# Moving three positions in the issue order of a hybrid attention and expert-retrieval layer: ScalarE's stage work, one weight load, three transposes

## The reference, cut to what matters

```python
# mixer: differential attention and causal pooling, merged by gates
h = x @ w_in                                  # q, k, v, p (pooling input), g (gates)
a = softmax(q1 k1) - lam * softmax(q2 k2)     # 8 heads, causal, ALiBi bias
attn = rms_norm(a @ v) @ w_attn_proj
pool = (multiscale_pool(p) @ pool_w) * pool_scale @ w_pool_proj
h1 = layer_norm(ALPHA * x + (g_attn * attn + g_pool * pool) @ w_out)
# PEER: 8 heads choose 16 of 16384 experts for each token
s = (h1 @ w_q) . sub_keys                     # two halves of 128 scores for each head
idx, gate = top-16 of the sums of two top-16 lists, softmax
act = gelu(u[idx] . h1)
out = layer_norm(ALPHA * h1 + sum(gate * act * v[idx]))
```

## Time and profile before

| | |
|---|---|
| median of 3 runs | 3181.0 us (3175.33 to 3182.49) |
| the profiled execution, its own time | 3174.81 us |
| its span in the trace | 3173.0 us |
| mean granted TensorE clock | 0.959 |
| PE busy | 2873.1 us (91%) |
| DVE busy | 2479.3 us (78%) |
| ACT busy | 964.8 us (30%) |
| POOL busy | 920.2 us (29%) |
| chain that ended last | PE 61%, DVE 20%, DMA 12%, issue 4%, ACT 2% |

### The profile page before, as it was taken

One profiled execution on the slowest core, in us unless ns is written; L12 is line 12 of the kernel. 1 busy time (PEld: TensorE's weight loads), 2 busy tenths in 40 slices (PEclk: granted clock), 3 DMA queues, 4 the chain that ended last, 5 costly groups with the idle time before them and its releaser, 6 DMA issues.

```text
span 3173.0 us, 31535 instructions
## 1 busy us (share of the span) xinstructions
PE 2873.1 (91%) x9793; PEld 1685.4 (53%) x9793; DVE 2479.3 (78%) x5164; ACT 964.8 (30%) x2683; POOL 920.2 (29%) x866
## 2 busy tenths in 40 slices
PE   9999999997698888967988888888999999999997
PEld 7785666553354555533555656333455545555553
DVE  2114678889898999899879998677877878877877
ACT  2311466611224556411235644111111111111110
POOL 1101234433333445433100012222333333333331
PEclk9999999998899999998999988999999999999999
DMA  5735889899999889899646479999999999999995
GB/s 184 256 105 188 325 301 338 311 393 364 417 392 360 326 303 332 328 408 381 250 138 235 164 258 340 390 386 394 414 398 406 403 394 404 392 413 413 402 404 196
DMA packets 225446, 1047.41 MB, mean 330 GB/s; under 512 B 23424, under 2 KB 70016, under 8 KB 141440
## 3 DMA queue, kind: packets, MB, share of 16 engines
q0 software_dynamic: 92160, 671.13, 53.9%
q1 hardware_dynamic: 132112, 374.13, 31.9%
q10 hardware_dynamic: 1008, 0.14, 0.0%
HBM read 995.50 MB, written 49.81 MB: 329 GB/s over the span
## 4 chain that ended last, share of the span: by engine, by line
PE 61%; DVE 20%; DMA 12%; issue 4%; ACT 2%; SPq 1%; POOL 0%; DVEq 0%; POOLq 0%; ACTq 0%
PE w_ps L1901 15%; PE w_ps L1669 12%; PE r_o L1915 12%; PE w_ps L1915 6%; DVE z_e L1556 5%; DVE ring L1598 4%; PE r_o L1847 3%; PE r_o L1669 3%; DMA ring<-uv,idx 3%; DMA gel_kept<-e_scr 2%; DVE hot_r L1478 2%; PE w_ps L1809 1%; DMA ub<-uT 1%; PE w_ps L1847 1%; PE r_o L1754 1%
## 5 line engine op out<-in xcount | busy, mean ns | idle before, releaser
L919 POOL DMA_INDIRECT ring<-uv,idx x640 | 762.6, 1192 | 1937.5 <-DVE z_e L1556 1872.0
L1556 DVE SCALAR_TENSOR_TENSOR z_e<-ring,coef,z_e 128x1024 f32<-128x1024 f32 x640 | 818.4, 1279 | 202.5 <-ACT coef L1153 202.1
L1598 DVE CUSTOM_DVE_ANT_0 ring<-ring,ytok 128x1024 f32<-128x1024 f32 x640 | 777.7, 1215 | 20.5 <-DMA ring<-uv,idx 20.1
L1901 PE MATMUL w_ps<-yT,ub 128*128 128x384 f32 x2048 | 693.3, 493 | 7.6 <-DMA ub<-uT 7.6
L1901 PEld LDWEIGHTS w_ps<-yT,ub 128*128 128x128 f32 x2048 | 393.6, 194 | 297.5 <-issue 52.6
L1669 PE MATMUL w_ps<-x,w 128*128 128x384 f32 (+1 forms) x1632 | 487.2, 446 | 8.2 <-DMA x<-xT 6.2
L1669 PEld LDWEIGHTS w_ps<-x,w 128*128 128x128 f32 x1632 | 303.5, 192 | 146.9 <-issue 26.8
L1915 PE MATMUL r_o<-vb,gel_d 128*128 128x512 f32 x704 | 318.2, 595 | 4.8 <-DMA vb<-v 4.8
L1130 ACT ACTIVATE gel_d<-w_ps 128x384 f32<-128x384 f32 x92 | 45.1, 490 | 767.4 <-PE w_ps L1901 767.4
L1149 ACT ACTIVATE gel<-dot 128x2 f32<-128x2 f32 x320 | 64.0, 200 | 645.9 <-DVE dot L1598 645.3
L1915 PEld LDWEIGHTS r_o<-vb,gel_d 128*128 128x128 f32 x704 | 134.4, 191 | 155.9 <-issue 127.2
(11 more groups left out here) (251 smaller groups left out, 3306.7 us busy)
## 6 DMA issues: line engine op xcount, KB each, us to landing
w<-w_in SPq DMA_DIRECT2D x132, 512.0 KB, 5.4
ub<-uT SPq DMA_DIRECT2D x128, 512.0 KB, 7.9
vb<-v SPq DMA_DIRECT2D x128, 512.0 KB, 9.9
g_scr<-stage_g SPq DMA_DIRECT2D x12, 2048.0 KB, 7.3
gq<-g_scr SPq DMA_DIRECT2D x16, 1536.0 KB, 24.7
wq<-wq SPq DMA_DIRECT2D x46, 512.0 KB, 7.8
wc<-w_branch SPq DMA_DIRECT2D x24, 768.0 KB, 8.4
wo<-w_out SPq DMA_DIRECT2D x24, 512.0 KB, 11.7
```

What stands on the lines that cost most here:

```text
L919: nc.gpsimd.indirect_dma_start(out=ring[t % RING][:], out_offset=None, in_=a["uv"], in_offset=bass.IndirectOffsetOnAxis(ap=idx[:, slot:slo ...
L1556: nc.vector.scalar_tensor_tensor(z[n % 2][:], ring[t % RING][:, D:], coef[:, slot:slot + 1], z[n % 2][:], ALU.mult, ALU.add).then_inc(vsum ...
L1598: nc.vector.tensor_tensor_reduce(ring[r][:, 0:D], ring[r][:, 0:D], y_of(n)[:], 1.0, 0.0, ALU.mult, ALU.add, dot[:, slot:slot + 1]).then_in ...
L1901: ins = nc.tensor.matmul(dense_bank(b)[:, 0:DENSE], ub[b % NUB][:, c], yT[2][c // 4][:, c % 4, :], start=c == 0, stop=c == DC - 1)
```

## The change

```diff
@@ SyncE, tokens(g) @@
             else:
-                yield norm_at(1, GTS[1]) + 15
+                yield score_at(1, 5)
                 sp.wait_ge(y1_out, 16 * len(PARKED))
             sp.dma_start(pw_raw[g][:], a["pool_w"]).then_inc(pw_in, 16)
@@ ScalarE, the loop over the slots @@
             for slot in range(0, SLOTS, GROUP):
                 coefficients(n, slot)
-                advance(tick_at(SLOTS * n + slot + GROUP))
+                advance(tick_at(SLOTS * n + slot + GROUP) + 5)
@@ TensorE, rcg_turns @@
             for i in range(DT):
-                yield TURN_AT[i]
+                yield TURN_AT[i] + 2
                 pe.wait_ge(share_step, 2 * i + 2)
```

## The result

The changed kernel takes **3271.4 us** (median of 4 runs, 3269.6 to 3276.3) against 3178.2 us for the kernel before in the same series. The ratio is 1.0295, with an interval of 1.0279 to 1.0310: about 94 us slower, 89 to 99. The forecast was 3230 us. The direction was right; the loss is nearly twice the forecast's 49 us.

The account below looks back on a forecast made before the run. VectorE was taken to bound stage 2's attention, stage 1's scores and the gate table, TensorE stage 1's attention and the tail. Terms 42 + 6 - 4 + 5 = +49 us on 3181.0 gave 3230 us, range 3178 to 3285.

Parts of the forecast that it names:

- Attention of stage 2, +42 us: Stage 2's attention: exponentials ahead of coefficients make VectorE wait, 34 us in 11 steps and 8 us in 6.
- the lower end: Stage 2's attention: VectorE's 25.5 idle us swallow part of the 42 us of new waits, leaving 16.5 us.
- the upper end: Stage 2's attention: ScalarE's 34.6 us of waits for value products are all handed on, growing it by 77 us.
- the one worked step: Stage 2's attention, slot 202: VectorE's add waits for its coefficient, 3.0 us late, 3.6 with two copies in between.
- Attention of stage 1, +6 us: Stage 1's attention: 14 us of late coefficients, covered by VectorE's idle time; gain at most 6.8, loss up to 28.
- Pooling weights, -4 us: Scores ahead of stage 2's attention: the later load frees SyncE's queue and shortens TensorE's wait; ends -12.1 and +3 us.
- Transpositions, +5 us: Transpositions of the shares: VectorE waits some 5.2 us longer at the first tile, nothing late at others; ends 0 and +5.
- Tail, 0 (-3 to +3): Dense tail: TensorE bounds it and VectorE has 200 us to spare, so ScalarE's lead costs nothing.
- Absorbed: Attention of stage 2: late coefficients fit VectorE's idle time and freed waits gain 19 us, giving 3162 us; chance 0.15.
- everything cancels: Whole kernel: 16.5 us left in stage 2's attention offset by 19 us won elsewhere, giving 3179 us; chance 0.09.
- The window is too narrow: Both attentions: TensorE's lateness passes through ScalarE to VectorE and back, +116 us, giving 3297 us; chance 0.14.
- the forecast's own case: Whole kernel: the summed terms hold, +49 us to 3230 us, within 3195 to 3265; chance 0.62.

Follow-up runs that it names:

- three ticks: Kernel before with ScalarE's work issued three ticks ahead everywhere, nothing else changed; ratio 0.9999 to the kernel before.
- five ticks, one slot more: Kernel before with ScalarE five ticks ahead and VectorE adding each slot one slot later (LAG 4 instead of 3); ratio 0.9991 to the kernel before.
- no table loads: Kernel before with ScalarE five ticks ahead and tanh replacing GELU in gather slots below 252, so output differs; ratio 1.0061 to the kernel before.
- four ticks: Kernel before with ScalarE's work issued four ticks ahead everywhere, nothing else changed; ratio 1.0050 to the kernel before.
- exponentials two ahead: Kernel before with ScalarE five ticks ahead, but the exponentials of stages 1 and 2 only two ahead; ratio 1.0428 to the kernel before.
- ScalarE alone: Kernel before with ScalarE five ticks ahead, pooling weights and transpositions left where they were; ratio 1.0274 to the kernel before.
- the slots of stage 1: Kernel before with ScalarE five ticks ahead only for gather slots under 72, stage 1's scores and attention; ratio 1.0176 to the kernel before.
- the exponentials alone: Kernel before with only the exponentials of stages 1 and 2 due five ticks earlier, ScalarE's other work in place; ratio 1.0520 to the kernel before.

## Why the prediction was right or wrong

**Attention of stage 2, +42 us: right in place and mechanism, in size partly by luck.** It grew by 46.0 us. The new coefficient waits are 59.1 us instead of 42, with 22 places of 2.7 us on average where the prediction had 11 of 3.1 and 6 of 1.3. VectorE's other waits fell from 19.8 us to 5.1, so 44 us of the new ones lengthened the stretch. Some idle time was swallowed, as the lower end had it, and lateness of TensorE was handed on (25.7 us behind transpositions), as the upper end had it. That the two would cancel was a choice that happened to hold; the 3.45 us of the one worked step was a reading that held.

**Attention of stage 1, +6 us: the step that failed.** It was +40.5 us. Two parts of the step were wrong. The count took a group for late only where a maximum stands close ahead of it, 5 steps and 14 us. But all 24 late results stand behind TensorE's products: ScalarE's waits for TensorE in this stage, where TensorE is the bound, grew from 94 to 143 us, because copies that it issues earlier are copies at which it stands. And the step took VectorE's 58.3 us of idle time for cover. 47 us of that were waits for ScalarE itself. Adding VectorE's waits for exponentials and for coefficients in stage 1 shows what it was:

| kernel | waits for both, us | growth of the stretch, us |
|---|---|---|
| before | 47.2 | 0 |
| three ticks | 51.4 | 0 |
| five ticks, one slot more | 54.2 | +1.9 |
| no table loads | 57.7 | +5.9 |
| four ticks | 62.4 | +9.9 |
| changed | 91.6 | +40.5 |
| exponentials two ahead | 153.4 | +103.6 |

VectorE's busy time is the same 221 to 223 us in all seven and its other idle time a few us, so by arithmetic alone the stretch must grow as these waits do. What the table adds is that there was next to no other idle time: above some 50 us each us of waiting is a us of time. The cause is shown by the runs with ScalarE alone, with the slots of stage 1 and with one slot more. (The kernel with the exponentials alone ahead is left out: there VectorE waits for TensorE's logits.) The exponentials did come earlier, as the prediction said (their waits went from 47.2 to 2.4 us), but the wait had moved behind them in the same queue and grown. TensorE, which had waited 3.9 us for VectorE to take logits, then waited 29.2 us; with 10.6 us of added busy time at the lower clock and 6.5 us of waits for mixed tiles that is 42 us, near the stretch's 40.5.

**Branches and norms, not in the sum: +18 us.** The prediction costed the lead only in the attentions and the tail. Four adds wait 15.7 us for coefficients in the branches of stage 1, two wait 11.1 us in those of stage 2; with the slots of stage 1 alone ahead, its branches take 8 us more.

**Pooling weights, -4 us: 0 (-5 to +6).** The interval holds the forecast too. All three waits went as described; of the gain, 6.9 us were taken up by gathered rows on DMA engines that were fully busy, which the earlier trace rows showed and the step did not use.

**Transpositions, +5 us: +5 (-1 to +10).** Right in place and size as far as the interval tells: 7.7 us of wait at the first tile where 7 were forecast, TensorE's waits for shares 5.4 us in two pieces. In the changed kernel it is hidden by the 8 us that ScalarE's lead gains in the scores of stage 2, which the prediction did not have either.

**Tail, 0 (-3 to +3):** -5 us in the trace. Over all the traces the kernels with five ticks there are some 11 us shorter than the others (see "Where the loss is made"), beyond the term's ends; the trace of the kernel before is the shortest of those others. The prediction looked at coefficients and gates alone, and what differs is TensorE's waits for dense rows. How the lead acts on them is open.

**The rivals.** "Absorbed" and "everything cancels" rested on VectorE's idle time as cover and fell with it. "The window is too narrow" had the right mechanism for stage 1 (TensorE's lateness handed on through ScalarE to VectorE, and VectorE's back to TensorE) and its stage 1 price, 28 us, was still too low. The measured 3271 us lies between it and the forecast's own case of 3195 to 3265, and inside the range of 3178 to 3285 only because that range took in a part of this rival. The sum was 49 us where 94 were measured: the one large term that held is stage 2's, and the gains in the tail and in the scores of stage 2, which it did not have, hid a part of what it missed in stage 1 and in the branches.

## What to carry to other kernels

When an in-order engine is given a lead, ask for each of its results how early it was before: a row in which the engine waits for its *input* at that result (here 50.8 us at the GELUs of stage 2, 10.9 in stage 1) is slack. Its disappearance says only that the result now hangs on something else: with three ticks the row was gone too, and that cost nothing. The loss is read from the consumer, here the adds that wait for coefficients. Count as cover only the consumer's own work between the input and the use, and against it put the last wait plus all that is queued between, whichever engine that wait is for. Idle time of a consumer that is itself a wait for the engine you are reordering is no cover: it is the same chain under another name.

## What the runs showed of the hardware

The same products took TensorE 272.2 us of busy time at a granted clock of 0.99 and 282.8 us at 0.94 in stage 1 (297.1 at 0.96, 312.7 at 0.91 in stage 2). In the same stretches TensorE waits more between its products: 29.2 us in stage 1 and 54.9 us in stage 2 for VectorE to take logits, against 3.9 and 17.5 us. The waits come first. The clock of the changed kernel's stage 1 falls to the lower level seven times, each time right behind the start of a wait of TensorE for VectorE. The first time that wait is this one, and the clock of the stretches around it (columns as in the earlier trace rows) goes from 0.99 to 0.51 and back to 1.00:

```profile
369.09 0.80 PE L1715 MATMUL w_ps<-k,q 64*128 64x128 f32 x4 [5.35 <-DVE st_a L1273]
360.50:367.30 6.80, 3.24 (x11) 1.57 (x9) 5.76 (x17) 1.92 (x6) 1.83 (x2) 0.99 0.98 324
367.30:374.10 6.80, 5.01 (x22) 4.58 (x22) 3.15 (x9) 2.12 (x8) 0.04 (x1) 0.51 0.94 368
374.10:381.00 6.90, 6.90 (x26) 4.17 (x25) 6.60 (x18) 3.33 (x7) 2.75 (x4) 1.00 0.52 169
```

The stretch with the most idle TensorE, stage 2 with the exponentials alone ahead, had 0.84. So a late coefficient on VectorE costs a second time, on an engine that it does not touch. No run changed the clock by itself.

With the table loads gone ScalarE's busy time in stage 2 is 133.8 us instead of 193.5; for the 45 loads left out that is 1.3 us each. The Trainium skill (ScalarE: Activation LUTs, What ACT_TABLE_LOAD costs) adds a drain of about 1380 ns to a switch; here the load starts 0.02 us behind the end of the copy before it (1242.49 + 0.35 and 1242.86 in the timeline above) and the GELU 0.01 us behind the load's end (1242.86 + 1.28 and 1244.15), so these runs show the load and no drain on either side of it.
